# Diagonals two slots ahead, stores two slots later, one query per step: a two-layer transformer kernel

## The reference

```python
def peer_ffn(h, w_q, sub_keys, u, v):
    k = PEER_TOPK                       # 16
    def block(xt):                      # 128 tokens
        q = (xt @ w_q).reshape(TOKEN_BLOCK, PEER_HEADS, 2, PEER_HALF_DIM)
        sc = jnp.einsum('thcd,chnd->thcn', q, sub_keys)
        top_s, top_i = lax.top_k(sc, k)
        ...
        best_s, best_pos = lax.top_k(cand_s.reshape(...), k)
        idx = jnp.take_along_axis(cand_i.reshape(...), best_pos, axis=-1)
        g = jax.nn.softmax(best_s, axis=-1)
        pre = jnp.einsum('td,thkd->thk', xt, u[idx])
        coef = g * jax.nn.gelu(pre)
        return jnp.einsum('thk,thkd->td', coef, v[idx])
```

## Time and profile before

| | us |
|---|---|
| median of 3 runs | 2663.78 |
| lowest, highest | 2653.27, 2674.37 |
| profiled execution, its own time | 2658.7 |
| its span | 2656.9 |
| PE busy | 2101.0 (79 %) |
| DVE busy | 1728.9 (65 %) |
| POOL busy | 1033.2 (39 %) |
| ACT busy | 606.6 (23 %) |
| granted TensorE clock, mean | 0.883 |

### The profile page before, as it was taken

The page is one execution under the profiler, slowest core; times in us unless marked ns, Lnnn a source line. Parts: engine busy times, 40 slices in busy tenths (PEclk is TensorE's granted clock), DMA queues, the critical chain, the costliest instruction groups (busy, mean ns, idle before and its releaser), DMA issues. The chain is left out here.

```text
span 2656.9 us, 25394 instructions
## 1 busy us (share of the span) xinstructions
PE 2101.0 (79%) x7625; PEld 1323.9 (50%) x7625; DVE 1728.9 (65%) x3556; ACT 606.6 (23%) x1394; POOL 1033.2 (39%) x1083
## 2 busy tenths in 40 slices
PE   4975857788765876775788777878787799799999
PEld 4954544444332334442344333333336774688877
DVE  4956338887877775567777587877847462544465
ACT  2134213342222111121212033222211230211121
POOL 0000015666666665566666466666750000000000
PEclk9985878989888988998999888888897897899999
DMA  5741038999999999899999899999984300333222
GB/s 176 288 143 64 17 127 300 357 341 364 355 337 409 356 369 360 303 355 359 371 402 403 318 371 347 361 364 331 380 326 151 112 10 0 111 95 95 79 79 95
DMA packets 266857, 676.48 MB, mean 255 GB/s; under 512 B 25725, under 2 KB 114162, under 8 KB 266738
## 3 DMA queue, kind: packets, MB, share of 16 engines
q0 software_dynamic: 147456, 536.94, 53.8%
q1 hardware_dynamic: 119282, 138.13, 15.6%
HBM read 672.87 MB, written 2.10 MB: 254 GB/s over the span
## 5 line engine op out<-in xcount | busy, mean ns | idle before, releaser
L2172 PE MATMUL bank<-arena 128*128 128x512 f32 x1536 | 816.1, 666 | 289.3 <-issue 120.6
L2402 DVE SCALAR_TENSOR_TENSOR arena<-arena,h_ps 128x1024 f32<-128x1024 f32 x512 | 612.5, 1216 | 175.8 <-DMA arena<-in_peer_u,arena 136.3
L2135 POOL DMA_INDIRECT arena<-in_peer_v,arena x512 | 511.4, 999 | 396.7 <-PE bank L2172 195.0
L2172 PEld LDWEIGHTS bank<-arena 128*128 128x128 f32 x1536 | 299.6, 209 | 640.0 <-issue 544.2
L2135 POOL DMA_INDIRECT arena<-in_peer_u,arena x512 | 506.6, 989 | 223.4 <-issue 143.5
L2415 DVE SCALAR_TENSOR_TENSOR x<-arena,x 128x1024 f32<-128x1024 f32 x128 | 164.5, 1285 | 48.0 <-DMA arena<-in_peer_v,arena 29.4
L1455 PE MATMUL bank<-hT,arena 128*128 128x256 f32 x512 | 134.7, 424 | 44.3 <-DMA arena<-in_peer_w_q 36.2
L2256 ACT ACTIVATE arena<-ident,arena 128x128 f32<-128x128 f32 x384 | 136.3, 394 | 78.1 <-PE bank L2172 36.1
L1455 PEld LDWEIGHTS bank<-hT,arena 128*128 128x128 f32 x512 | 109.4, 216 | 76.7 <-DMA arena<-in_peer_w_q 40.4
L142 DVE CAST parts<-arena 128x2048 fp32r<-128x2048 f32 (+4 forms) x60 | 68.1, 1136 | 112.1 <-DMA arena<-in_w_gate_up 72.7
L144 DVE TENSOR_TENSOR parts<-arena,parts 128x2048 fp32r<-128x2048 f32 (+4 forms) x60 | 126.7, 2111 | 4.5
(11 more groups left out here) (412 smaller groups left out, 3340.7 us busy)
## 6 DMA issues: line engine op xcount, KB each, us to landing
arena<-in_w_in SPq DMA_DIRECT2D x16, 1536.0 KB, 6.8
arena<-in_w_ada SPq DMA_DIRECT2D x12, 2048.0 KB, 9.7
arena<-in_w_gate_up SPq DMA_DIRECT2D x44, 512.0 KB, 5.0
arena<-in_peer_w_q SPq DMA_DIRECT2D x16, 1024.0 KB
arena<-in_w_down SPq DMA_DIRECT2D x22, 512.0 KB, 3.5
arena<-in_peer_u,arena POOLq DMA_INDIRECT x512
arena<-in_peer_v,arena POOLq DMA_INDIRECT x512
arena<-in_w_in SPq DMA_DIRECT2D x8, 1024.0 KB
```

The lines of the kernel that those rows point to most:

```text
L2135: nc.gpsimd.indirect_dma_start(out=ring[:, n % R, :], out_offset=None, in_=a[table][0], in_offset=bass.IndirectOffsetOnAxis(ap=expert[:, s ...
L2172: ins = nc.tensor.matmul(psum[half][:, :], diag[:, m % R, :], v_ring[:, n % R, half * 512:(half + 1) * 512], start=(s % PH == 0 and j == 0 ...
L2402: nc.vector.scalar_tensor_tensor(out=u_ring[:, n % R, :], in0=u_ring[:, n % R, :], scalar=1.0, in1=h_ps[:, :], op0=ALU.mult, op1=ALU.mult, ...
```

## The change

Four edits.

1. `query_due`: queries 8 to 15 run one in each of the steps 12 to 19, the halves in slots 1 and 4, the scores in slot 6. SP's order gets w_in_2 tile 2 between w_q 14 and w_q 15.
2. `spread`: ScalarE makes the diagonals of slot j + 2 in slot j (SPREAD_AHEAD = 2), and those of slots 0 and 1 at slot 0 (slot 2 is VectorE's).
3. `offsets`: `store_out` of `att_b` at 4u + 9 instead of 4u + 7, `store_out2` of `att2_a` at 3u + 9 instead of 3u + 8.
4. Block 2 leaves bank 6 to the queries. `gate_rows` uses banks 4 and 5 and no longer waits for `sc_copied`; the transposes and the input tiles go through banks 4, 5, 7 in turn. A tile's 256 tokens are no longer done side by side: slots 0 to 3 of its phase do the first 128 tokens (two k each), slots 4 to 7 the second, and each half is copied out by itself (`in2_part`, `in2_half`). Tile 8 waits for all copies, tile 9 (bank 6) for `sc_copied`.

```diff
@@ -1239,7 +1239,7 @@
-        att_b = att_places(1, 4, (0, 1, 2, 3, 4, 5, 6, 7),
+        att_b = att_places(1, 4, (0, 1, 2, 3, 4, 5, 6, 9),
@@ -1425,6 +1425,7 @@
         DVE_J = (2, 6, 10, 14)
+        SPREAD_AHEAD = 2
@@ -1442,9 +1443,7 @@
             if i < PH - 3:
                 return [(i + 3, 1)]
-            if 12 <= i < 16:
-                return [(PH + 2 * (i - 12), 0), (PH + 2 * (i - 12) + 1, 8)]
-            return []
+            return [(i - 12 + PH, 1)] if 0 <= i - 12 < PH else []
@@ -1915,7 +1915,7 @@
-        att2_a = att2_places(0, 3, (0, 1, 2, 3, 4, 5, 7, 8), 2, psum[4:6], [psum[7]] * 2, psum[6],
+        att2_a = att2_places(0, 3, (0, 1, 2, 3, 4, 5, 7, 9), 2, psum[4:6], [psum[7]] * 2, psum[6],
@@ -1926,32 +1926,41 @@
+        IN2_BANKS = [psum[4], psum[5], psum[7]]
+
+        def in2_bank(t, b):
+            return IN2_BANKS[(2 * t + b) % 3]
+
         def block2_pe(pe, slot):
             if slot == 1:
                 pe.wait_ge(b_copied, 2 * KD)
-                pe.wait_ge(sc_copied, 2 * PH)
-                gate_rows(pe, G1)
+                gate_rows(pe, G1, psum[4:6])
...
-                pe.wait_ge(b_copied, 2 * KD + max(k - 3, 0))
+                pe.wait_ge(b_copied, 2 * KD + max(k - 2, 0))
                 for b in range(2):
-                    ins = nc.tensor.transpose(psum[4 + k % 4][:, b * P:(b + 1) * P], rows[:, b, k * P:(k + 1) * P], ident[:, :])
+                    ins = nc.tensor.transpose(IN2_BANKS[k % 3][:, b * P:(b + 1) * P], rows[:, b, k * P:(k + 1) * P], ident[:, :])
...
-                after(pe, in2_copied, t - 1)
+                after(pe, in2_copied, min(t - 1, 8) if t < 8 else 8)
+                if t == 9:
+                    pe.wait_ge(sc_copied, 2 * PH)
             if 0 <= t < 8:
-                n = TILES_2[t][1]
-                for b in range(2):
-                    ins = nc.tensor.matmul(psum[4 + t % 2 * 2 + b][:, 0:n], hT_of[0][:, k, b * P:(b + 1) * P], tile_2(t)[:, k, :],
-                                           start=(k == 0), stop=(k == KD - 1))
+                n, b = TILES_2[t][1], k // 4
+                if k == 4:
+                    after(pe, in2_half, t)
+                for kk in range(k % 4 * 2, k % 4 * 2 + 2):
+                    ins = nc.tensor.matmul(in2_bank(t, b)[:, 0:n], hT_of[0][:, kk, b * P:(b + 1) * P], tile_2(t)[:, kk, :],
+                                           start=(kk == 0), stop=(kk == KD - 1))
+                if k == 3:
+                    ins.then_inc(in2_part, 1)
@@ -2003,21 +2012,22 @@
-            t, k = (slot - I0) // KD - 1, (slot - I0) % KD
+            t, k = (slot - I0) // KD, (slot - I0) % KD
+            if 0 <= t < 8 and k == 4:
+                act.wait_ge(in2_part, t + 1)
+                nc.scalar.copy(proj2_dst(0, t)[:, 0, :], in2_bank(t, 0)[:, 0:TILES_2[t][1]]).then_inc(in2_half, 1)
+            t -= 1
             if 0 <= t < 10 and k == 0:
                 act.wait_ge(in2_summed, t + 1)
                 if t < 8:
-                    n = TILES_2[t][1]
-                    for b in range(2):
-                        ins = nc.scalar.copy(proj2_dst(0, t)[:, b, :], psum[4 + t % 2 * 2 + b][:, 0:n])
-                    ins.then_inc(in2_copied, 1)
+                    nc.scalar.copy(proj2_dst(0, t)[:, 1, :], in2_bank(t, 1)[:, 0:TILES_2[t][1]]).then_inc(in2_copied, 1)
@@ -2120,7 +2130,9 @@
                         for t in range(2):
                             load_w_2(sync, t)
-                for t in range(2, len(TILES_2)):
+                    if Q == 2 * PH - 2:
+                        load_w_2(sync, 2)
+                for t in range(3, len(TILES_2)):
                     load_w_2(sync, t)
@@ -2320,8 +2332,9 @@
                             if j == 0:
                                 gelus(i - 1)
-                            if j not in DVE_J:
-                                spread(i - 1, j)
+                            for m in range(0 if j == 0 else j + SPREAD_AHEAD, min(j + SPREAD_AHEAD + 1, PK)):
+                                if m not in DVE_J:
+                                    spread(i - 1, m)
```

More of the change, by code:

```diff
@@ L1535, in program @@
         w_2_loaded, in2_summed, in2_copied = [sem("w_2_even"), sem("w_2_odd")], sem("in2_summed"), sem("in2_copied")
+        in2_part, in2_half = sem("in2_part"), sem("in2_half")
         gates_zeroed, bias_loaded, places_ready = sem("gates_zeroed"), sem("bias_loaded"), sem("places_ready")
@@ L1568, in load_w_out_a, with gate_rows @@
             sync.dma_start(w_out_a[i], w_out_all[:, k0:k0 + w_out_a[i].shape[1], :]).then_inc(w_out_loaded, 16)
-        def gate_rows(pe, g0):
+        def gate_rows(pe, g0, banks):
             for k in range(KD):
-                ins = nc.tensor.matmul(psum[6 + k // 4][:, k % 4 * P:k % 4 * P + P],
+                ins = nc.tensor.matmul(banks[k // 4][:, k % 4 * P:k % 4 * P + P],
                                        mod[:, g0 + k:g0 + k + 1].to_broadcast([P, P]), ident[:, :], start=True, stop=True)
@@ L1937, in block2_pe @@
                     pe.wait_ge(b_normed, 8)
-                if k == 2:
                     pe.wait_ge(g_copied, 1)
-                pe.wait_ge(b_copied, 2 * KD + max(k - 3, 0))
+                pe.wait_ge(b_copied, 2 * KD + max(k - 2, 0))
                 for b in range(2):
-                    ins = nc.tensor.transpose(psum[4 + k % 4][:, b * P:(b + 1) * P], rows[:, b, k * P:(k + 1) * P], ident[:, :])
+                    ins = nc.tensor.transpose(IN2_BANKS[k % 3][:, b * P:(b + 1) * P], rows[:, b, k * P:(k + 1) * P], ident[:, :])
                 ins.then_inc(b_turned, 1)
@@ L2005, in block2_act @@
                 for i in range(2):
-                    ins = nc.scalar.copy(gate_row[:, i * 512:(i + 1) * 512], psum[6 + i][:, :])
+                    ins = nc.scalar.copy(gate_row[:, i * 512:(i + 1) * 512], psum[4 + i][:, :])
                 ins.then_inc(g_copied, 1)
@@ L2010, in block2_act @@
                 act.wait_ge(b_turned, 2 * KD + k + 1)
-                nc.scalar.activation(hT_of[0][:, k, :], psum[4 + k % 4][:, 0:GT], ACT.Identity, scale=mod_gain[:, k:k + 1],
+                nc.scalar.activation(hT_of[0][:, k, :], IN2_BANKS[k % 3][:, 0:GT], ACT.Identity, scale=mod_gain[:, k:k + 1],
                                      bias=mod[:, SH1 + k:SH1 + k + 1]).then_inc(b_copied, 1)
-            t, k = (slot - I0) // KD - 1, (slot - I0) % KD
+            t, k = (slot - I0) // KD, (slot - I0) % KD
[3 more added lines that the diff above has]
+            t -= 1
             if 0 <= t < 10 and k == 0:
@@ L2780, in _ @@
             def _(pe):
-                gate_rows(pe, G2)
+                gate_rows(pe, G2, psum[6:8])
                 with pe.Fori(0, KF // 2) as i:
```

## The result

| | before | after |
|---|---|---|
| median of four runs, us | 2663.23 (2653.27 to 2674.37) | 2633.02 (2626.99 to 2636.80) |
| ratio after / before, 95 % interval | | 0.989 (0.9851 to 0.9929) |
| profiled execution, us (span) | 2658.7 (2656.9) | 2626.99 (2625.2) |

What follows compares the result with a forecast made beforehand. The loop was taken as DMA-bound, 354 GB/s against 403, 198 us lost, with TensorE holding up the gathers. -23 + 2 - 11 + 0 + 0 = -32 from 2658.7 gives 2626.7; median 5.1 above, 2632 us; range 2604 to 2664.

Steps and rivals of the forecast that it cites:

- Part 1: Steps 12 to 19: one query per step ends the waits for w_q; lost time 47 to 24 us, gain 23.
- upper bound: Part 1, steps 12 to 19: spread loads fill the holes in six of the eight steps; gain 40 us.
- Part 2: Step 19: w_q 15 behind w_in_2 tile 2 makes TensorE wait 2 to 12 us; cost 2, bounds 0 and 12.
- Part 3: Whole loop: diagonals two rows ahead cut TensorE's waits from 113.7 to near 50 us; gain 11, bounds 0 and 57.
- The fifth that the text took of the waits: Part 3: of 57 us of diagonal waits a fifth counts, 11 us, since the ring of six hides most.
- Part 4: Attention steps: later stores end VectorE's waits, some 65 us, but TensorE waits on stores; 0 us, bounds -25 and +20.
- The text called itself wrong: If POOL's wait for TensorE rises in steps 1 to 8 and 24 to 29, or steps 16 to 19 grow over 5 us each.
- Rival C: At turn_q and score2, later stores hold TensorE; 22 to 56 us reach POOL, 2654 to 2688 us; chance 0.09.
- Part 5: Block 2: three banks, same matmuls and copies, tile 8 waits 0.5 us for tile 7's copy; 0 us.
- Rival A: Moved work costs as much where it lands, the ring hides diagonals; gain 4 to 20, about 2650 us; chance 0.24.
- Rival B: Whole loop: at a limit of the memory, no reordering moves it; 2664 us; chance 0.06.
- Rival D: Step 19: w_q 15 holds TensorE the full 12 us and POOL twice as long; 2652 us; chance 0.05.

Runs made afterwards that it cites:

- eleventh experiment: Kernel before with one query per step, three banks and w_q 15 issued before w_in_2 tile 2; diagonals, stores, gate weights as before: 2625.98 us, ratio 0.9883, slow chip.
- fourth experiment: Kernel before with a second w_q buffer for queries 11, 13 and 15, still two queries a step: 2542.41 us, ratio 0.9923, fast chip.
- third: Changed kernel with w_q 15 issued before w_in_2 tile 2: 2537.23 us, ratio 0.9903 to the kernel before, fast chip.
- tenth: The ninth with diagonals two rows ahead and later stores: 2590.14 us, ratio 0.9737 to the kernel before, slow chip.
- second: Changed kernel with diagonals and stores put back, queries and banks alone: 2542.07 us, ratio 0.9915 to the kernel before, fast chip.
- sixth: Kernel before with diagonals two rows ahead and nothing else: 2566.01 us, ratio 1.0003, fast chip.
- fifth experiment: Kernel before, unchanged, run once for its profile on the fast kind of chip: 2569.88 us.
- experiments 1 to 8: The follow-up runs made on two chips of the fast kind, where the kernel before takes 2567 us; medians 2524.49 to 2571.02 us.
- eighth kernel: Kernel before with one query per step, three banks, w_q 15 first, gate weights in their own place after tile 3: 2524.49 us, ratio 0.9836, fast chip.
- ninth: The eighth kernel with gate weights loaded ahead of w_in_2 tiles 0 and 1: 2604.91 us, ratio 0.9796 to the kernel before, slow chip.

## Why the prediction was right

The time was right and its main cause too. Part of the hit is luck: the queries gave more than forecast, the other parts less, and the errors cancelled. The cleanest split is on the slow kind of chip, on which the forecast was made. The eleventh experiment holds parts 1 and 5 alone: 31.8 us, where 23 were forecast. So parts 2 to 4 together cost 1.6 us (30.2 instead of 31.8), where the forecast had them gain 9. Each of these times is uncertain by some 10 us, so the split is rough; the steps (at the end of this section) go the same way.

**Part 1, one query per step: right in mechanism, low in size.** Forecast: 47 us lost over steps 12 to 19, 24 afterwards. Counted in the same way (length less bytes at 403 GB/s), steps 12 to 18 lost 47.4 us before and 14.8 after, 2.1 each and not 3. They became 37.5 us shorter; the 4.9 beyond the lost time are bytes that went to step 19 and out of the stretch. The late load is the cause: with two buffers and all else unchanged steps 13 to 15 were 30 us shorter (fourth experiment). The term that was mis-sized is the loss of the steps that hold one query and one load, taken as 3 us each. Steps 14, 15 and 16 ran at 400, 405 and 398 GB/s, where 403 means no loss. The text had this case as its upper bound ("if the spread loads fill the holes as in steps 19 to 21"), and three steps of the eight met it. Steps 12 and 18 still lost 4.4 and 5.7.

**Part 2, w_q 15 behind w_in_2 tile 2: the wait was right, its price was not.** Forecast: a wait of 2 to 12 us, at a cost of 2. The wait was 7.05 us, and step 19 grew by 10.5. Some 2.7 us of it are bytes (62 us at 350 GB/s are 21.7 MB, has 20.6 in step 19; 1.1 MB at 403). The other 8 are lost time, 8.2 us where the forecast had 3 + 2; that the wait and the slow half query behind it make them up is argued from the timeline. The price of the order as the runs give it: 7 to 11 us on the fast kind (third), 13.8 us in step 19 alone on the slow kind (eleventh). The failing step is "in a stretch at 403 GB/s where the gathers have work queued": that was the stretch of before. POOL's longest wait, 12.1 us, ended at 1314.96 us, after 7.05 us of TensorE's, as in the earlier trace rows, where 5.87 us of TensorE went with 10.96 of POOL. The price of a TensorE stall was in the rows and was not used.

**Part 3, diagonals: the waits as forecast, the price open between 0 and 15.** Waits near 50 us instead of 113.7 were forecast, those left at slot 0; 46.2 were measured, all at slot 0, where the text had counted 44. The 11 us stand against -0.7 on the fast chip and, with the stores and the open question of slot 0, 14.8 on the slow one (tenth), most of it in steps 22 to 24. In the changed kernel itself the steps without queries moved by 4 us in all against before, but by 9 us against the eleventh. The fifth that the text took of the waits rests on one step, and no run shows it: 32 to 43 us of waits outside slot 0 went for nothing visible on the fast kind (second and sixth).

**Part 4, stores: right, with one sign against it.** 0 us, bounds -25 and +20; +4.3 measured on the fast chip. The waits before the stores went, 71 us and not the 65 of the text. TensorE's on the stores came, 14.0 us at turn_q where 18 were forecast and 7.1 in steps 24 to 29 where 16 were. The text called itself wrong if POOL's wait for TensorE in steps 1 to 8 and 24 to 29 rose: in the second stretch it did, by 9.3 us, with those steps 1.7 us longer. Rival C wanted 22 to 56 us and is out.

**Part 5, banks: right.** -0.8 us.

**The sum.** Forecast -23 + 2 - 11 + 0. Measured in the steps of the two profiles: about -37.5 for steps 12 to 18, +10.5 for step 19, -4 for all others; 31. Over steps 12 to 19 that is 27 us against a forecast of 21, for all others 4 against 11. The text's other sign of being wrong, steps 16 to 19 growing by more than 5 us each, came in step 19 alone.

Rival A (5.4 us lost in every step with a load) fails at steps 14 to 16, which lost 0.5, -0.2 and 0.6. Rival B, a limit of the memory near 358 GB/s, fails at the same rows and at 409 GB/s in the fifth experiment. The Trainium skill's figure in DMA: Bandwidth & Descriptors, Bandwidth, about 358 GB/s for one core, is passed there by 14 %; the same section gives it as each core's part when both cores of a pair stream, and here one core ran. The Trainium skill, DMA: Bandwidth & Descriptors, Issuing engines are not separate DMA queues, has all transfers run on the same 16 engines and interleave, from which the prediction concluded that a moved load costs its bytes wherever it goes. This agrees with the fast chip, where steps 16 to 18 moved 5.3 MB more (13 us at 403 GB/s) and grew by 11.4 us, and not with the slow one, where they moved 4.2 MB more (10 us) and grew by 3.5: bytes are cheap where the gathers leave holes. Rival D was half true: POOL's wait in step 19 went from 8.5 to 18.3 us.

## What to carry to other kernels

A load that lands late in front of the engine that frees the ring costs more than its wait: here 7 us of TensorE went with 12 us of POOL and 8 us of lost time. Three such faults were worth about 24 us (w_q in steps 13 to 15), 7 to 14 us (w_q 15) and 13 to 21 us (the gate weights). Look first at what stands ahead of such a load in the issuing queue and whether a second place lets it start earlier; a second place took off 24 us with no work moved, and the order of two transfers 7 us or more. Spread loads over steps that have holes, expect to pay their bytes in steps that have none, and try a gain of 1 % on more than one chip.

## What the runs showed of the hardware

**Two kinds of chip.** The kernel before took 2567 us on two chips (experiments 1 to 8) and 2658 to 2663 on the chip of the others and in the first runs. That it is the chip, and nothing else that differed between these runs, is the plainest reading and not shown. The loop has the same bytes; on the first kind it took 1529.8 us, on the second 1618.1. Steps with plain transfers run at 403 GB/s on both, and the steps of gathers alone that are shown at 397 and 409 against 348 and 357. On the faster kind POOL issues one gather behind the other, every 1.25 us (timeline of POOL, step 25 there):

```profile
1603.12 0.95 POOL L2135 DMA_INDIRECT arena<-in_peer_v,arena  x1 [0.30 <-issue]
1604.37 0.94 POOL L2135 DMA_INDIRECT arena<-in_peer_u,arena  x1 [0.30 <-issue]
1605.62 0.94 POOL L2135 DMA_INDIRECT arena<-in_peer_v,arena  x1 [0.31 <-issue]
```

So the 32 gathers of a step take 40 us to issue, and steps 24 to 27 there took 40.5 to 41.5: they are about as short as POOL's own pace lets them be, and an edit to the waits has little to win in them (an estimate from these rows). That is one reason why diagonals and stores may show nothing on that kind.

On the slower kind POOL also waits between gathers, 72.6 us of the loop for a releaser that the trace doesn't name. The other kernels on that kind have such waits too (72.7 us after, 82.2 in the eleventh), those on the faster kind have none. The mean granted clock was 0.901 against 0.883 over the execution, which makes TensorE slower, but step 16 had 0.92 at 348 GB/s on the slow kind and step 17 0.84 at 397 on the fast one, so the clock alone doesn't explain it. The cause stays open.

**It may turn small verdicts round.** Queries without diagonals and stores were 6 us faster than with them on the fast kind, which is within the noise, and in the kernel with the gate weights first 15 us slower on the slow kind, which is not. Chip and kernel changed together here, and the tenth lacks waits that the edits don't touch, so what makes it faster is not shown. The fast kind alone would have thrown the edits away.

**Small pieces.** The three transfers of the gate weights, 16 to 24 KB each, kept SP's queue for 23.50 us in the eighth kernel, 18.40 in the ninth and 9.94 in the third. The longest of these is more than the 17.7 us from issue to landing of a tile of 1536 KB beside the gathers (list of DMA issues, fifth experiment, 1362 to 1412 us).
